# The rows of the last routed pass go to the output by a product with a matrix of zeros and ones

## The reference, cut to what matters

```python
y_slots = lax.map(expert_block, (slot_tok..., slot_w..., block_e))     # (hid @ we_down[e]) * ws
routed = jax.ops.segment_sum(y_slots..., slot_tok, num_segments=N + 1)[:N]
shared = (jax.nn.silu(uf @ ws_gate) * (uf @ ws_up)) @ ws_down
...
h = h + g2[:, None, :] * (routed + shared)
return rmsnorm(h, final_norm_g)
```

## Time and profile before

| | us |
|---|---|
| median of 3 runs (2220.75 to 2223.47) | 2223.23 |
| the profiled execution | 2225.7 |
| its span, from the first to the last instruction | 2223.5 |
| end of the last pass's products on TensorE, from the start of the span | 2189.97 |
| first load of `y_halves` issued | 2197.83 |
| last store of the output issued | 2220.75 |

### The profile page before, as it was taken

One profiled execution on the slowest core, in us unless ns is written; L12 is line 12 of the kernel. 1 busy time (PEld: TensorE's weight loads), 2 busy tenths in 40 slices (PEclk: granted clock), 3 DMA queues, 4 the chain that ended last, 5 costly groups with the idle time before them and its releaser, 6 DMA issues.

```text
span 2223.5 us, 31527 instructions
## 1 busy us (share of the span) xinstructions
PE 2134.8 (96%) x11794; PEld 1533.8 (69%) x11795; DVE 1208.6 (54%) x1881; ACT 718.4 (32%) x1124; POOL 731.0 (33%) x459
## 2 busy tenths in 40 slices
PE   6999999999989999999999999999999989999895
PEld 5877567787868777777777778876655555555453
DVE  5566555789981448599999593256321212121122
ACT  5335563333342334344444355123111111111012
POOL 4331023434443324333333356431122222222220
PEclk9999799999999999999999999999999999999998
DMA  4230122454534212333333322322779899999984
GB/s 164 76 95 1 67 77 76 147 194 152 195 137 149 97 60 79 103 104 100 100 105 100 90 67 104 129 84 100 280 233 347 288 328 326 306 337 323 321 271 146
DMA packets 165678, 359.04 MB, mean 161 GB/s; under 512 B 12080, under 2 KB 101296, under 8 KB 146768
## 3 DMA queue, kind: packets, MB, share of 16 engines
q1 hardware_dynamic: 143360, 304.00, 38.5%
q0 software_dynamic: 15232, 39.02, 7.4%
q10 hardware_dynamic: 6992, 14.75, 1.9%
HBM read 340.87 MB, written 33.62 MB: 168 GB/s over the span
## 4 chain that ended last, share of the span: by engine, by line
PE 86%; DMA 5%; ACT 3%; DVE 3%; POOL 1%; issue 1%; SPq 0%; ACTq 0%; POOLq 0%; DVEq 0%
PE bank L902 24%; PE bank L1634 14%; PE bank L1325 12%; PE bank L1655 7%; PE bank L1224 4%; PE bank L1404 3%; DMA arena<-in_we_gate 2%; PE bank L1613 2%; PE bank L1038 1%; PE bank L1411 1%; DMA arena<-in_w_up 1%; PE bank L1489 1%; PE bank L1073 1%; PE bank L911 1%; PE bank L919 1%
## 5 line engine op out<-in xcount | busy, mean ns | idle before, releaser
L1634 PE MATMUL bank<-arena,hn 128*64 128x256 f32 x3072 | 345.0, 383 | 13.7 <-DMA arena<-in_we_gate 12.8
L1634 PEld LDWEIGHTS bank<-arena,hn 128*64 128x64 f32 x3072 | 232.1, 139 | 138.8 <-issue 43.8
L800 POOL TENSOR_TENSOR w_low_flat<-arena,in_high 128x1024 fp32r<-128x1024 f32 x71 | 184.4, 2618 | 278.4 <-ACT in_high L1951 278.3
L2904 DVE TENSOR_TENSOR inv<-inv,bank 128x128 f32<-128x128 f32 x96 | 23.3, 284 | 327.4 <-PE bank L1634 327.4
L1655 PE MATMUL bank<-arena 128*64 128x512 f32 x768 | 175.4, 598 | 5.0 <-DVE arena L2910 0.5
L767 POOL TENSOR_TENSOR w_low<-arena,w_high 128x2048 fp32r<-128x2048 f32 x22 | 103.8, 4719 | 160.8 <-ACT w_high L1873 160.8
L2918 DVE SCALAR_TENSOR_TENSOR sq<-bank,arena 128x512 f32<-128x512 f32 x96 | 72.1, 751 | 151.2 <-PE bank L1655 149.4
L1325 PE MATMUL bank<-in_x,in_high 128*128 128x512 f32 x384 | 154.2, 402 | 0.0
L1325 PE MATMUL bank<-in_x,w_low_flat 128*128 128x512 f32 x384 | 151.1, 393 | 0.0
L1325 PE MATMUL bank<-x_low,in_high 128*128 128x512 f32 x384 | 150.7, 392 | 0.0
L902 PE MATMUL bank<-x_high,w_high 128*128 128x512 f32 x336 | 133.4, 397 | 2.6 <-POOL w_low L767 2.6
(11 more groups left out here) (494 smaller groups left out, 4875.8 us busy)
## 6 DMA issues: line engine op xcount, KB each, us to landing
arena<-in_we_gate SPq DMA_DIRECT2D x49, 1024.0 KB
arena<-in_we_up SPq DMA_DIRECT2D x49, 1024.0 KB
arena<-in_we_down SPq DMA_DIRECT2D x49, 1024.0 KB
arena<-in_w_in SPq DMA_DIRECT2D x38, 1024.0 KB, 5.4
arena<-in_w_ada SPq DMA_DIRECT2D x12, 2048.0 KB, 8.0
arena<-in_w_up SPq DMA_DIRECT2D x22, 1024.0 KB, 10.8
arena<-in_w_in SPq DMA_DIRECT2D x17, 512.0 KB, 5.3
arena<-in_w_out SPq DMA_DIRECT2D x4, 2048.0 KB, 10.0
```

Source lines behind the costliest of these rows:

```text
L800: pool_eng.tensor_tensor(in2_tile(j, "low"), in2_tile(j, "whole"), in2_tile(j, "high").bitcast(f32), ALU.subtract).then_inc(S("w_low"), 1)
L1634: ins = nc.tensor.matmul(rows_of(banks[2 + part][:, 0:FE], c), columns_of(moe["xT"][:, p, :], k, c), moe["gu"][:, 2 * p + c, at:at + FE], ...
```

## The change

The last pass is no longer scattered. The loads of `y_rows` wait for the scatter of the last pass but one alone. GpSimd copies the last pass's token numbers to `LAST_TOKENS` (a column), VectorE compares them with the token numbers of each tile and gets `LAST_PICK`, four 128 x 128 matrices with a one where a slot belongs to a token (in a free part of lane 0 of `moe["dn"]`). TensorE multiplies `moe["y"]` by them after the last pass: eight f32 products of 128 x 128 by 128 x 512 into the eight banks, which are the last pass's rows by token. The two loaded parts are now added by GpSimd, a tile at a time, and `last_h` on VectorE adds the bank's rows to that sum in two halves. ScalarE takes the four squares and roots first and then the second halves of tiles 0 and 2; VectorE does the other six half tiles. Five semaphores of VectorE become one, `vector_made`, counted up; those edits are left out below, since they move no instruction.

```diff
@@ -303,7 +303,10 @@
         moe.update(lay(late["end"] + 2 * KD * P, g2=(D,)))
+        LAST_OUT = [(0, 0), (1, 0), (1, 1), (2, 0), (3, 0), (3, 1)]
         LAST_SUM = ROW_SUM[:, 0:TT]
+        LAST_TOKENS = moe["shift"][:, 1:2]
+        LAST_PICK = moe["dn"][:, 0, D:D + T].rearrange("p (t n) -> p t n", n=P)
         LAST_INV = sq[:, :, 0:P]
         u32, i32 = mybir.dt.uint32, mybir.dt.int32
...
@@ -702,15 +706,16 @@
             for p in range(2):
-                sp.wait_ge(S(f"y_added{p}"), pairs * 16 + 16)
+                sp.wait_ge(S(f"y_added{p}"), pairs * 16 + 16 * (1 - p))
             for tt in range(TT):
                 for n in range(2):
                     sp.dma_start(acc[n][:, tt, :], y_rows[n * Y_ROWS + tt * P:n * Y_ROWS + (tt + 1) * P, :])\
                       .then_inc(S(f"panel_in_slot{tt}"), 16)
             for tt in range(TT):
-                for half, (done, value) in enumerate((("norm_out", KD * NORM_OUT["n6"]), ("half_out", 0))):
-                    sp.wait_ge(S(done), value + tt + 1)
+                for half in range(2):
+                    sp.wait_ge(*((S("half_out"), tt // 2 + 1) if half == 1 and tt % 2 == 0 else
+                                 (S("norm_out"), KD * NORM_OUT["n6"] + LAST_OUT.index((tt, half)) + 1)))
                     sp.dma_start(out_T[4 * half * P:4 * (half + 1) * P, tt * P:(tt + 1) * P].rearrange("(k p) n -> p k n", p=P),
                                  hn[:, 4 * half:4 * half + 4, tt * P:(tt + 1) * P]).then_inc(S("stored"), 16)
             sp.wait_ge(S("stored"), 16 * 2 * TT)
...
@@ -882,8 +887,12 @@
                 weights(i * 2, 0)
             scatter(pairs_but_one * 2 + (-1), 1, pairs)
             weights(pairs_but_one * 2 + 1, 1)
+            pool_eng.tensor_copy(LAST_TOKENS, moe["idx"][:, bass.ds(pairs_but_one * 2 + 1, 1)]).then_inc(S("w_known"), 1)
             scatter(pairs_but_one * 2, 0, pairs)
-            scatter(pairs_but_one * 2 + 1, 1, pairs + 1)
+            for tt in range(TT):
+                pool_eng.wait_ge(S(f"panel_in_slot{tt}"), counted[tt] + 32)
+                pool_eng.tensor_tensor(acc[0][:, tt, :], acc[0][:, tt, :], acc[1][:, tt, :], ALU.add)\
+                        .then_inc(S("rows_added"), 1)
         @block.tensor
         def _(pe):
...
@@ -1682,6 +1691,14 @@
             block_down(pairs_but_one * 2 + 1, 1)
+            pe.wait_ge(S("vector_made"), VECTOR_MADE["last_pick"])
+            for tt in range(TT):
+                for half in range(2):
+                    if tt == 0:
+                        pe.wait_ge(S("y_copied"), pairs_but_one * 4 + (2 * TT + 3 + half))
+                    nc.tensor.matmul(banks[2 * tt + half][:, :], LAST_PICK[:, tt, :],
+                                     moe["y"][:, 1, 512 * half:512 * half + 512], start=True, stop=True)\
+                      .then_inc(S("acc_T"), 1)
             for tt in range(TT):
                 pe.wait_ge(S("norm_inv"), NORMS["n6"] + tt + 1)
...
@@ -2254,7 +2271,7 @@
             def last_half(tt):
-                act.wait_ge(S("acc_T"), 2 * tt + 2)
+                act.wait_ge(S("acc_T"), 2 * TT + 2 * tt + 2)
                 for q in range(4):
                     ins = nc.scalar.activation(hn[:, 4 + q, tt * P:(tt + 1) * P], banks[2 * tt + 1][:, q * P:(q + 1) * P],
                                                ACT.Copy, scale=col("final_norm", 4 + q))
...
@@ -2267,9 +2284,8 @@
                 act.wait_ge(S("norm_sq"), KD * NORMS["n6"] + tt + 1)
                 nc.scalar.activation(RECIP[:, tt:tt + 1], LAST_SUM[:, tt:tt + 1], ACT.Sqrt, bias=EPS_COLUMN, scale=1.0 / D)\
                   .then_inc(S("norm_root"), 1)
-                if tt >= 1:
-                    last_half(tt - 1)
-            last_half(TT - 1)
+            for tt in (0, 2):
+                last_half(tt)
         @block.vector
...
@@ -2934,14 +2950,22 @@
                     block_hidden(b, p)
                     block_hidden_T(b, p)
                     block_out(b, p, added)
+            dve.wait_ge(S("w_known"), pairs_but_one * 2 + 3)
+            for tt in range(TT):
+                ins = nc.vector.tensor_scalar(LAST_PICK[:, tt, :], iota, LAST_TOKENS, float(-P * tt), ALU.subtract, ALU.is_equal)
+            ins.then_inc(S("vector_made"), 1)
             block_hidden(pairs_but_one * 2 + 1, 1)
             block_hidden_T(pairs_but_one * 2 + 1, 1)
             block_out(pairs_but_one * 2 + 1, 1, pairs)
             def last_h(tt):
-                dve.wait_ge(S(f"panel_in_slot{tt}"), counted[tt] + 32)
-                nc.vector.tensor_tensor(acc[0][:, tt, :], acc[0][:, tt, :], acc[1][:, tt, :], ALU.add).then_inc(S("h_done"), 1)
+                dve.wait_ge(S("rows_added"), tt + 1)
+                for half in range(2):
+                    dve.wait_ge(S("acc_T"), 2 * tt + half + 1)
+                    part = acc[0][:, tt, 512 * half:512 * half + 512]
+                    ins = nc.vector.tensor_tensor(part, part, banks[2 * tt + half][:, :], ALU.add)
+                ins.then_inc(S("h_done"), 1)
             def last_inverse(tt):
...
@@ -2950,22 +2974,25 @@
                 nc.vector.tensor_scalar(LAST_INV[:, tt, :], ident, RECIP[:, tt:tt + 1], None, ALU.mult)\
                   .then_inc(S("norm_inv"), 1)
-            def last_out(tt):
-
-                dve.wait_ge(S("acc_T"), 2 * tt + 1)
-                nc.vector.tensor_tensor(hn[:, 0:4, tt * P:(tt + 1) * P], banks[2 * tt].rearrange("p (k n) -> p k n", n=P),
-                                        col("final_norm", 0, 4).unsqueeze(2).to_broadcast([P, 4, P]), ALU.mult)\
+            def last_out(tt, half):
+
+                dve.wait_ge(S("acc_T"), 2 * TT + 2 * tt + half + 1)
+                nc.vector.tensor_tensor(hn[:, 4 * half:4 * half + 4, tt * P:(tt + 1) * P],
+                                        banks[2 * tt + half].rearrange("p (k n) -> p k n", n=P),
+                                        col("final_norm", 4 * half, 4).unsqueeze(2).to_broadcast([P, 4, P]), ALU.mult)\
                   .then_inc(S("norm_out"), 1)
             last_h(0)
             last_h(1)
             last_inverse(0)
-            for tt in range(TT):
-                if tt + 2 < TT:
-                    last_h(tt + 2)
-                if tt + 1 < TT:
-                    last_inverse(tt + 1)
-                last_out(tt)
+            last_h(2)
+            last_inverse(1)
+            last_h(3)
+            last_inverse(2)
+            last_out(*LAST_OUT[0])
+            last_inverse(3)
+            for tt, half in LAST_OUT[1:]:
+                last_out(tt, half)
 # ---- launch: one core; kernel() lays the inputs out ----
```

More of the change, by code:

```diff
@@ L337, in two_blocks @@
                                                          "plan_in_rows"))}
+        VECTOR_MADE = {name: n + 1 for n, name in enumerate(("selected", "keys_made", "new_runs", "plan_made", "last_pick"))}
         PREPARED = {"halved": 0, "lam_dot": 1, "subln": 3, "neg_lam": 4, "tables": 5}
@@ L1528, in counts @@
             def counts():
-                pe.wait_ge(S("selected"), 1)
+                pe.wait_ge(S("vector_made"), VECTOR_MADE["selected"])
                 sel = moe["sel"].rearrange("p t e -> p (t e)")
@@ L1541, in ranks @@
             def ranks():
-                pe.wait_ge(S("keys_made"), 1)
+                pe.wait_ge(S("vector_made"), VECTOR_MADE["keys_made"])
                 nc.tensor.matmul(banks[3][:, (TT + 2) * E:(TT + 3) * E], ones[0:E, :], pcol("order")[0:E, 0:E], start=True,
@@ L1547, in run_counts @@
             def run_counts():
-                pe.wait_ge(S("new_runs"), 1)
+                pe.wait_ge(S("vector_made"), VECTOR_MADE["new_runs"])
                 nc.tensor.matmul(banks[3][:, 0:1], tri, pcol("new"), start=True, stop=True).then_inc(S("pe_made"), 1)
             def plan_in_rows():
-                pe.wait_ge(S("plan_made"), 1)
+                pe.wait_ge(S("vector_made"), VECTOR_MADE["plan_made"])
                 for j, name in enumerate(("expert", "lane", "free")):
@@ L2772, in _ @@
             steps_done()
-            nc.vector.tensor_scalar(flat(moe["sel"]), flat(moe["left"]), -1e38, None, ALU.is_lt).then_inc(S("selected"), 1)
+            nc.vector.tensor_scalar(flat(moe["sel"]), flat(moe["left"]), -1e38, None, ALU.is_lt).then_inc(S("vector_made"), 1)
             for tt in range(TT):
@@ L2793, in _ @@
             nc.vector.tensor_scalar(pcol("order")[0:E, 0:E], keys[0:E, :], pcol("own_key")[0:E, :], pcol("own_halves")[0:E, :],
-                                    ALU.is_lt, ALU.mult).then_inc(S("keys_made"), 1)
+                                    ALU.is_lt, ALU.mult).then_inc(S("vector_made"), 1)
             step(nc.vector.tensor_reduce(pcol("pairs"), moe["nb"], AX.X, ALU.add))
@@ L2825, in _ @@
             step(nc.vector.tensor_tensor(pcol("first"), pcol("pos"), pcol("fourth"), ALU.is_lt))
-            nc.vector.tensor_tensor(pcol("new"), pcol("new"), pcol("first"), ALU.mult).then_inc(S("new_runs"), 1)
```

(3 more changed lines are left out.)

## The result

| | before | after |
|---|---|---|
| median, us | 2221.36 (2215.37 to 2223.47, 6 runs) | 2207.3 (2203.91 to 2217.84, 6 runs) |
| the profiled execution, us | 2225.7 | 2209.77 |
| its span, us | 2223.5 | 2207.8 |
| end of the last pass's rows on VectorE | 2190.7 | 2184.3 |
| from there to the end of the span | 32.8 | 23.5 |

The ratio is 0.9944 (95% interval 0.9927 to 0.9961). The fourth row of the table says where to look: 6.4 of the 15.7 us between the two spans were there already when the last pass's rows were made, and only the last row, 9.3 us, is the end of the program. From here on "the rows' end" is that moment, the end of VectorE's last scaling, and "the end" is what follows it.

A forecast was written before the change was run, and what follows sets the result against it. The prediction saw the end as one string of waits, its bandwidth-bound loads starting late. Earlier loads (12.1 us) less additions in series (2.6) gave 9.5 at h(3), 9.7 with the stores' queue: median 2213.5, range 2210.5 to 2217.0.

The forecast's parts named there:

- Earlier loads, 12.1 us: Loads at the end wait for the scatter issued at 2179.50 instead of 2191.62, so they move 12.12 us earlier.
- rival (3): The last-but-one pass's scatter lands 12.0 us after issue, not 6.15; gain only 3.8 us; chance 0.05.
- (5): Something else holds SyncE, so the loads start no earlier; median 2225.6, no change; chance 0.02.
- GpSimd's additions, 2.37: GpSimd's four new 128 x 1024 additions, on the path, take 2.37 us each after their tile's landing.
- Rival (2)'s first half: GpSimd's additions take 2.96 us, moving h(3) and the stores by 1.4; gain 8.3; chance 0.20 for both halves.
- rival (4): GpSimd's four additions in series make the kernel slower, if above 5.1 us each; chance 0.03.
- TensorE's product, 7.1, hidden: TensorE's eight f32 products with ones after the last pass take 7.1 us and cost nothing on the path.
- TensorE's clock stays up: Between the product with ones and tile 0's norm products, a 1.2 us gap leaves TensorE at full clock.
- second half of rival (2): TensorE's clock falls, norm products take 3.35 us each, span ends at 2215.2; gain 8.3; chance 0.20 for both halves.
- Stores set the end: Seven stores queue behind tile 0's second half at 2205.5, 0.93 us each, ending the span at 2213.8.
- Rival (1): The output stores do not queue; span ends at 2211.0, 12.5 us less, median 2210.7; chance 0.10.
- Sum, 9.7 us: Over the end of the program, the span falls from 2223.5 to 2213.8, 9.7 us less.

The follow-up runs named there:

- old names: The changed kernel with the old four semaphores instead of `vector_made`, same instructions, transfers and waits; ratio 0.9943 to the kernel before.
- shifted: The changed kernel with 16 empty instructions at the start of TensorE's, ScalarE's and VectorE's programs; ratio 0.9945 to the kernel before.
- loads late: The changed kernel, but SyncE also waits for VectorE to make the last pass's rows before loading; ratio 0.9969 to the kernel before.
- additions on VectorE: The changed kernel with the two loaded parts added on VectorE instead of GpSimd; ratios 0.9951 and 0.994 to the kernel before.
- the half tile earlier: The changed kernel with ScalarE's half of tile 0 ahead of the last square; ratios 0.9948 and 0.9946 to the kernel before.
- the stores sooner: The changed kernel with additions on VectorE, and ScalarE taking both halves of tile 0 between its squares; ratios 0.9952 and 0.9935 to the kernel before.

## Why the prediction was wrong

What it said of the loads, the additions and the stores held, and the end became shorter by about what it gave; what it said of TensorE's clock held in some executions only, and the total lay outside the range.

- *Earlier loads, 12.1 us.* Counted from the rows' end, the first load was issued at -4.7 (forecast -5.0) and the tiles' additions began at 1.3, 3.8, 6.4 and 8.9 (forecast landings -0.1, 3.2, 5.8, 8.3). Right within 1.4 us, and h(3) was done at 12.6 (forecast 12.1); the scatter took 6.46 us, not 12.0, so rival (3) is out, and (5) with it. Putting the loads back behind the rows cost 4.9 us.
- *GpSimd's additions, 2.37.* 2.34 to 2.37 measured. Rival (2)'s first half and rival (4) are out. But the prediction looked for a disturbance of GpSimd alone, and among VectorE's work beside the additions it left out the diagonal. That took 1.23 us instead of 0.29. In all sixteen cases (two in each of the eight traces with additions on GpSimd) it ended 0.07 to 0.09 us behind the end of the addition beside it, and it took less (1.23 down to 1.18) by about as much as it began later. So it looks held until the addition was over, and not slowed in proportion; the starts differ by only 0.07 us, so that is a reading and not a test. The rule of the Trainium skill that the prediction cited (GPSIMD Engine Reference, Key points) says that the two engines share their SBUF interfaces, and names VectorE instructions with two SBUF operands or in a two-port mode. The Trainium skill (VectorE: DVE Perf Modes, Mode 2×_2P) says that an f32 instruction with one tensor from SBUF and a scalar can run in that mode. The trace agrees with both: L2974 was held up, `last_h` with its operand in a bank took 1.28 us for two additions with GpSimd at work and without. And the same form (L2398 in the kernel before) took 486 ns for 512 columns and 287 for 128, 0.52 ns a column, where additions of two SBUF tensors (L2944 and L2887) took 1225 ns for 1024 and 692 for 512, 1.04 a column. Which of the two engines waits, the rows showed.
- *TensorE's product, 7.1, hidden.* 7.13, and hidden.
- *TensorE's clock stays up.* Wrong in this profile: the gap was 2.5 us instead of 1.2, 0.9 of it the stretched diagonal, and PEclk fell to 0.50 for about 3 us, which the prediction had named as a sign of being wrong and, as the second half of rival (2), had priced at 1.4 us. Of the changed kernel's two other executions one had a gap of 1.6 us and kept 1.00, the other one of 2.0 us and fell. It cost nothing at the end: with the clock kept and with it lost, the span ended 8.2 to 8.3 us behind ScalarE's half of tile 0, as the next step has it.
- *Stores set the end.* The second store was issued at 15.2 (forecast 14.8), and seven stores from there with 8.3 us to the end (7 x 0.93 + 1.8) give 2207.8, the span. In seven more traces with this order of stores (the changed kernel twice, old names, shifted, loads late, additions on VectorE twice) it is 8.2 to 8.5 us, and with the half tile earlier and with the stores sooner the same sum from the third and the fourth store gives the span within 0.1. The last store here was issued at 2203.7, 4.1 us ahead of the end and not 2.75. Rival (1) is out.
- *Sum, 9.7 us.* 32.8 less 23.5 in the first pair of profiles, 9.3; with all three profiled executions of the changed kernel (23.0 on average) 9.8.

What failed is the last step, from the sum to the median and its range. The sum puts what lies ahead of the rows' end at no difference, starts from one median of three executions, 2223.2, and takes the range from the rivals: "the runs before lie 2.7 us apart, so I leave as much above it". Below rival (1)'s 2210.7 it leaves 0.2 us. Three runs happened to agree. With six, the median before was 2221.36, which is 1.9 of the 6.2 us missing; the other 4.3 are that the medians differ by 14.0 and not by 9.7. 82 executions of the kernel before have a standard deviation of 3.3 us and go from 2215 to 2230, and the changed kernel's six went from 2204 to 2218. An estimate from these 82: a median of three has a standard deviation of 2.2 us and one of six of 1.5, their difference 2.7. Two of these below 2210.7 are 2205.3, and 2207.3 would have been inside. So the miss is in part a draw, and the error was to leave no room for one.

Beyond that, 3 us stay. The changed kernel is 13.3 us below the kernel before (18 against 82 runs, standard error 0.9), 9.8 of them at the end and 0.4 outside the span (2.0 against 2.4 us). The remaining 3.1 are ahead of the end, and there is a second witness, an estimate: by the runs' mean granted clocks, 0.9894 against 0.9844, and less what is lost at the end itself (2.3 and 10.2 us), the changed kernel lost 21.0 us of clock ahead of the end and the kernel before 24.5. The version with the old names has them too (2184.2); the five other kernels with the new end, or nearly it, do not, the shifted one above all (2187.6). Over 75 executions with the new end and 140 with the old, the time ahead of it is 2185.7 against 2186.5, with standard errors of 0.4 and 0.3. So the gain of the end as such is shown, and the 3 us go with the changed kernel's own executions. Whether they are a draw or come with the place of its instructions (C), the runs do not settle. For C speaks that shifting took them from the changed kernel and gave 1.4 us to the kernel before, but both are within two standard errors, and by its ratio (0.9945) the shifted kernel is like the others. For a draw speaks that the seven means ahead of the end, 2183.8 to 2187.6, scatter only 1.2 times as much as kernels without any difference would.

## What to carry to other kernels

A wait for the last of a chain of transfers can be taken off the end of a program by computing the last member's share on chip: here a product with zeros and ones cost nothing, since TensorE would have stood idle, and it shortened the time in which the clock was low from some 20 us to some 3. Then the output stores are next, and their order decides: giving the first tile's halves to the engine that is idle first was worth 1.3 us. Measure such a change in the trace, from a landmark just ahead of it; the total time of this program moves by more from one execution to the next than the edits at its end. And when a median is forecast, take the spread from as many executions as there are, and leave it on both sides.

## What the runs showed of the hardware that was not expected

TensorE's granted clock in one and the same stretch of one program, 80 us of attention, ranged from 0.83 to 0.96 between executions, and in the first pair of profiles it alone was 6.4 us of time. A VectorE instruction of 128 x 128 that began beside one of GpSimd's additions ended 0.07 to 0.09 us behind it, after 1.18 to 1.23 us instead of 0.29, while the additions did not slow down at all (2.34 to 2.37 us). TensorE's clock fell behind gaps of 2.0 to 2.7 us in its work at the end in five traces and stayed at 1.00 in two with gaps of 1.6 and 1.7 us.
